# Plain fp32 matmuls for the first two column groups of the second projection, a staging buffer swapped, a bias fill moved, and the last tile reordered in a two-layer encoder

## What is computed

```
p = rmsnorm(x) @ w_in[l]            # mixer a | b | c | cross q | gate
layer 0:  o = softmax(q k^T * 64**-0.5 + bias[dist]) v      # own chunk of 64 and 8 before it
layer 1:  o = rmsnorm(recurrence(q, k, i, log_f))           # state 128 x 128 per head
y = concat(o, cross_attn(xq, mk, mv)) * silu(gate);   x = x + y @ w_out[l]
outputs: final rmsnorm(x), new keys and values, states, memory keys and values
```

## Time and profile before

| | us |
|---|---|
| median of 3 runs (2514.9 to 2525.43) | 2517.48 |
| the profiled execution, its own time | 2513.61 |
| its span, first to last instruction | 2511.7 |
| PE busy / DVE / ACT / POOL in the span | 2404.9 / 1863.4 / 1463.0 / 363.0 |
| mean granted TensorE clock | 0.986 of full |

### The profile page before, as it was taken

The page is one execution under the profiler, slowest core; times in us unless marked ns, Lnnn a source line. Parts: engine busy times, 40 slices in busy tenths (PEclk is TensorE's granted clock), DMA queues, the critical chain, the costliest instruction groups (busy, mean ns, idle before and its releaser), DMA issues. The chain is left out here.

```text
span 2511.7 us, 61163 instructions
## 1 busy us (share of the span) xinstructions
PE 2404.9 (96%) x23733; PEld 2126.7 (85%) x23733; DVE 1863.4 (74%) x3612; ACT 1463.0 (58%) x3337; POOL 363.0 (14%) x584
## 2 busy tenths in 40 slices
PE   8999999999989999999997899999999979999997
PEld 5999999999856777777776898999999968888885
DVE  7899787877655555555555999788798867888884
ACT  4555666655555555555554565676766656666663
POOL 1331000000012111111111232000000021212111
PEclk9999999999999999999999999999999989999998
DMA  6887887789883222222224788777779794443441
GB/s 233 286 294 247 275 277 243 229 249 301 244 250 93 78 62 79 70 72 84 76 77 153 241 292 277 239 250 245 238 252 293 250 277 120 123 139 114 135 129 66
DMA packets 402563, 480.61 MB, mean 191 GB/s; under 512 B 40516, under 2 KB 249212, under 8 KB 402280
## 3 DMA queue, kind: packets, MB, share of 16 engines
q1 hardware_dynamic: 385592, 416.51, 52.5%
q0 software_dynamic: 14848, 55.45, 6.5%
q10 hardware_dynamic: 1840, 4.75, 0.7%
HBM read 329.78 MB, written 151.56 MB: 192 GB/s over the span
## 5 line engine op out<-in xcount | busy, mean ns | idle before, releaser
L1406 PE MATMUL pj_acc<-x_hi,pj_wh 128*128 128x256 f32 (+1 forms) x3136 | 918.4, 293 | 32.7 <-DVE pj_wl L478 30.1
L1406 PE MATMUL pj_acc<-x_lo,pj_wh 128*128 128x256 f32 (+1 forms) x3136 | 906.7, 289 | 0.0
L1406 PE MATMUL pj_acc<-x_hi,pj_wl 128*128 128x256 f32 (+1 forms) x3136 | 906.7, 289 | 0.0
L471 ACT ACTIVATE pj_wh<-pj_wt 128x512 fp32r<-128x512 f32 x728 | 456.5, 634 | 347.5 <-DMA pj_wt<-tsum 251.3
L1406 PEld LDWEIGHTS pj_acc<-x_hi,pj_wh 128*128 128x128 f32 x3136 | 597.5, 191 | 46.3 <-DVE pj_wl L478 43.5
L1406 PEld LDWEIGHTS pj_acc<-x_hi,pj_wl 128*128 128x128 f32 x3136 | 597.9, 191 | 0.0
L1406 PEld LDWEIGHTS pj_acc<-x_lo,pj_wh 128*128 128x128 f32 x3136 | 597.6, 191 | 0.0
L478 DVE SCALAR_TENSOR_TENSOR pj_wl<-pj_wt,pj_wh 128x512 fp32r<-128x512 f32 x728 | 510.3, 716 | 112.6 <-ACT pj_wh L471 98.6
L1259 DVE TENSOR_TENSOR pj_out<-pj_out,pj_acc 128x512 f32<-128x512 f32 (+1 forms) x448 | 319.8, 714 | 87.1 <-PE pj_acc L1406 59.2
L2531 ACT COPY pb_pt<-pb_TP 128x384 f32<-128x384 f32 (+2 forms) x272 | 107.2, 394 | 296.7 <-PE pb_TP L2246 224.1
L2415 DVE COPY pb_pt<-pb_TP 128x256 f32<-128x256 f32 (+2 forms) x266 | 115.8, 435 | 146.7 <-PE pb_TP L2243 133.5
(11 more groups left out here) (341 smaller groups left out, 3872.0 us busy)
## 6 DMA issues: line engine op xcount, KB each, us to landing
pj_wt<-tsum SPq DMA_DIRECT2D x588, 256.0 KB, 3.5
proj<-pj_out SPq DMA_DIRECT2D x112, 512.0 KB, 4.2
tsum<-pj_wt SPq DMA_DIRECT2D x140, 256.0 KB, 3.3
pj_wraw<-in_w_in_dram POOLq DMA_DIRECT2D x24, 1024.0 KB, 6.5
tsum<-pj_wraw SPq DMA_DIRECT2D x56, 256.0 KB, 4.0
hg_x<-x_mid SPq DMA_DIRECT2D x17, 512.0 KB, 3.6
out_dram<-hg_x POOLq DMA_DIRECT2D x17, 512.0 KB, 3.0
pb_gate<-proj SPq DMA_DIRECT2D x16, 512.0 KB, 5.0
```

Source lines behind the costliest of these rows:

```text
L471: nc.scalar.mul(self.hi[j][:], self.source(step), scale_of(c, self.l)).then_inc(self.s_hi, 1)
L1406: ins = nc.tensor.matmul(BANK[j][:, 0:n], a[j][:, k], x.of(y, p, j)[:, k], start=(k == 0 and i == 0), stop=(k == 3 and i == 2))
```

## The change

Four edits, in three stages.

1. **Second projection.** `whole` = 14 steps (groups 0 and 1 of pass 0, layer 1 only) are done in plain fp32: four matmuls a step straight from the sums or raws of x and of the weights. For them no `hi` or `lo` of weights is made. The `hi` of x (terms 2 to 6) go into ACT's loop, the seven `lo` of x into DVE's loop (`LOWS`), each behind the last step that reads its sum. A sum's buffer may now be overwritten only when its store has landed (`s_tst`). The banks of the first transposes (`SPACE`) are permuted.
2. **Sample keys** are staged in the first six blocks of the second gate buffer `gt[1]` in place of `tT`; `load_values(1)` and `load_queries(1)` are issued before that store, the wait on `s_ko` stands before `load_gate(1)`.
3. **Bias fill** of tile 1 at pair MG = 6 in place of pair 3.
4. **Last tile of `prompt_hgrn`**: pieces 8 to 10 behind `outputs`, the others laid between updates and turns; the last job's first half goes to a free bank of `hg_SC`, its second half to `hg_OP`; DVE's state updates go behind `add` and `low_part`; the state's store is issued before the last powers; the last scale and the last store are in two halves, the store on SP.

```diff
+        self.whole = 2 * TERMS * l
@@ add, keep (the same line for sp in keep)
         wait(eng, self.s_mm, step - TERMS + 1)
+        if TERMS <= step < self.whole + TERMS:
+            eng.wait_ge(self.s_tst[j], 16 * c)
@@ low
-        dve.wait_ge(self.s_hi, step + 1)
+        dve.wait_ge(self.s_hi, step + 1 - self.whole)
@@ project
+    LOWS = {5: 1, 6: 3, 8: 0, 10: 2, 12: 4, 13: 5, 14: 6}
-        SPACE = [B1[:], B3[:], B4[:], B52[:, 0], B52[:, 1], B76[:, 0], B76[:, 1], TP[:]]
+        SPACE = [B76[:, 0], B76[:, 1], B1[:], B52[:, 1], B4[:], B52[:, 0], TP[:], B3[:]]
@@ load_raw
-                    pool.wait_ge(w.s_lo, TERMS * (c - 2) + 5)
+                    if TERMS * (c - 2) < w.whole:
+                        pool.wait_ge(w.s_mm, TERMS * (c - 2) + 5)
+                    else:
+                        pool.wait_ge(w.s_lo, TERMS * (c - 2) + 5 - w.whole)
@@ scalar
-                    for j in range(TERMS):
-                        x.high(nc, act, 0, j)
-                        w.high(nc, act, j)
+                    x.high(nc, act, 0, 0)
+                    x.high(nc, act, 0, 1)
...
+                    if l and 1 < t < TERMS:
+                        x.high(nc, act, 0, t)
-                    if t >= 2 and step < STEPS:
+                    if t >= 2 and w.whole <= step < STEPS:
                         w.high(nc, act, step)
@@ vector, in the loop (t = step)
+                    if l and t <= 10 and t in LOWS:
+                        first_low(t)
...
-                    if t >= 5 and step < STEPS:
+                    if t >= 5 and w.whole <= step < STEPS:
                         w.low(nc, dve, step)
+                    if l and t > 10 and t in LOWS:
+                        first_low(t)
@@ tensor
+                        if step < w.whole:
+                            ins = nc.tensor.matmul(BANK[j][:, 0:n], w.source(step)[:, k], x.source(0, j)[:, k],
+                                                   start=(k == 0), stop=(k == 3))
+                            continue
@@ prompt_band, sync
                 load_pair(7)
+                load_values(1)
+                load_queries(1)
...
-                sp.dma_start(v["a_k_sample"][0].rearrange("b s h d -> (b s) (h d)"), tT[:].rearrange("p g n -> p (g n)")
-                             ).then_inc(s_ko, 16)
+                sp.dma_start(v["a_k_sample"][0].rearrange("b s h d -> (b s) (h d)"), staged).then_inc(s_ko, 16)
                 load_weights(3)
-                sp.wait_ge(s_ko, 16)
-                load_values(1)
-                load_queries(1)
                 sp.wait_ge(s_sc, 2 * (PAIRS - 1))
                 load_keys(1)
+                sp.wait_ge(s_ko, 16)
                 load_gate(1)
-                    if T == 1 and p == 3:
+                    if T == 1 and p == MG:
@@ prompt_hgrn
+            return SC[bank(NT - 1, LEVELS - 1)] if (job, half) == (JOBS - 1, 0) else OP
-                            wait(pe, s_xadd, 2 * job + half)
+                            wait(pe, s_xadd, 2 * job if job == JOBS - 1 else 2 * job + half)
+                project(NT - 1, 8, LATE)
                 update(NT - 1, 0)
                 project(NT - 1, LATE, LATE + 2)
                 update(NT - 1, 1)
-                project(NT - 1, LATE + 2, CHUNKS)
                 turn_outputs(NT, 0)
+                project(NT - 1, LATE + 2, LATE + 4)
                 turn_outputs(NT, 1)
+                project(NT - 1, LATE + 4, CHUNKS)
                 project(NT, 0, CHUNKS)
```

More of the change, by code:

```diff
@@ L449, in keep @@
             self.loaded(sp, c)
+            if TERMS <= step < self.whole + TERMS:
+                sp.wait_ge(self.s_tst[j], 16 * c)
         else:
@@ L1300, in _ @@
                     w.add(nc, dve, 1)
-                    w.add(nc, dve, 3)
-                    x.low(nc, dve, 0, 0)
                     dve.wait_ge(x.s_raw, 8)
@@ L1396, in _ @@
                     q, n = pair(step), x.width(p)
-                    pe.wait_ge(w.s_lo, step + 1)
-                    if c == 0:
-                        pe.wait_ge(x.s_lo, TERMS * p + j + 1)
+                    if step < w.whole:
+                        if j in w.PLAIN:
+                            w.loaded(pe, c)
+                        else:
+                            w.summed(pe, c, j)
+                        if c == 0 and j in x.SUMS:
+                            pe.wait_ge(x.s_add, x.MADE[0][j])
+                    else:
+                        pe.wait_ge(w.s_lo, step + 1 - w.whole)
+                        if c == (w.whole // TERMS if p == 0 else 0):
+                            pe.wait_ge(x.s_lo, TERMS * p + (list(LOWS.values()).index(j) if l and p == 0 else j) + 1)
                     if j == 0 or j == 3:
@@ L2678, in bank, with sum_of @@
             return place_of[t, what] % 3
+        def sum_of(job, half):
+            return SC[bank(NT - 1, LEVELS - 1)] if (job, half) == (JOBS - 1, 0) else OP
         def blocks(a):
@@ L2718, in _ @@
                         load_x(t + 1)
+                for half in range(2):
+                    cs = slice(half * 512, half * 512 + 512)
+                    sp.wait_ge(s_out, JOBS + half)
+                    sp.dma_start(v["y_prompt"].rearrange("b (t p) d -> (b t) p d", p=P)[NT - 1][:, cs], xt[NT % 2][:, cs]).then_inc(s_last, 16)
+                sp.wait_ge(s_last, 32)
             @block.gpsimd
@@ L2767, in _ @@
                 power(NT - 1, 1)
-                for job in range(NT - 1, JOBS):
-                    final_power(job)
-                    store(job)
                 pool.wait_ge(s_state, 2 * NT)
                 pool.dma_start(v["b_state_prompt"][0, 0].rearrange("h k v -> k h v"), three(st[:])).then_inc(s_stx[1], 16)
-                pool.wait_ge(s_stx[0], 16 * (JOBS - JOBS // 2))
+                final_power(NT - 1)
+                store(NT - 1)
+                final_power(NT)
+                pool.wait_ge(s_stx[0], 16 * (JOBS - JOBS // 2 - 1))
                 pool.wait_ge(s_stx[1], 16 * (JOBS // 2 + 1))
@@ L3020, in add, with last_scale @@
                     cs = slice(half * 512, half * 512 + 512)
-                    nc.vector.tensor_tensor(xt[job % 2][:, cs], xt[job % 2][:, cs], OP[:], ALU.add).then_inc(s_xadd, 1)
+                    nc.vector.tensor_tensor(xt[job % 2][:, cs], xt[job % 2][:, cs], sum_of(job, half)[:], ALU.add).then_inc(s_xadd, 1)
+                def last_scale(half):
+                    at = NT % 2
+                    cs = slice(half * 512, half * 512 + 512)
+                    dve.wait_ge(s_ldf, 16)
+                    dve.wait_ge(s_frs, JOBS)
+                    nc.vector.scalar_tensor_tensor(out=xt[at][:, cs], in0=xt[at][:, cs], scalar=fr[:, at:at + 1], in1=fg[:, cs],
+                                                   op0=ALU.mult, op1=ALU.mult).then_inc(s_out, 1)
                 def final_mean(job):
```

45 lines of the change are left out of this document (21 added, 24 removed).

## The result

The changed kernel took 2488.8 us, the median of four runs (2482.83 to 2491.52). The kernel before took 2516.2 us beside it, so the ratio is 0.9903 with a 95% interval of 0.9884 to 0.9923: 27.4 us less, 19 to 29 by the interval. The profiled execution took 2482.83 us, with a span of 2481.1 us. The forecast was 2488.5 us. 22 lies in both intervals, 27 only in the first. That the first median came within 0.3 us of the forecast is therefore luck: the direction and most of the mechanism were met, but not every term behind the number.

A forecast was written before the change was run, and what follows sets the result against it. TensorE, busy 2404.9 of 2511.7 us, was taken as the bound. Gains of 9.0 + 3.7 + 8.3 + 6.0 = 27.0 us off a level of 2515.5 gave 2488.5 us, range 2479 to 2503.

The forecast's parts named there:

- start of the second projection: Second projection, steps 0 to 14: fp32 lets PE begin 5.7 us earlier and reach step 14 at 1404.9, gaining 9.0 us.
- band attention, tiles 0 and 1: Tile 0's wait for values goes (3.7 us), tile 1's wait behind POOL and half clock go (8.3 us): 12.0 us.
- end: After the last block copy: earlier last job, no gap between its halves, earlier stores; gain 6.0 us.
- The price of a step: Second projection: a plain fp32 step of four matmuls costs 2.14 us, 0.38 us more than the fp32r step.
- what is late next is `lo` for steps 16 and 17, about 1 us ahead of PE: Second projection after the fp32 steps: DVE's `lo` for steps 16 and 17 has about 1 us of slack.
- The first rival: Band attention: the load stays the limit, tiles 0 and 1 give 3.9 + 1.5 us, time 2495; chance 0.14.
- the two halves: Last job: with its own bank the 1.18 us between the halves becomes 0.24, gaining 0.95 us.
- The stores: End: state stored long before, SP issues the output halves, landing near 2506.4 instead of 2508.55, gaining 2.1 us.
- Everything else of PE's time the change leaves alone: Outside the second projection's start, band attention tiles 0 and 1 and the end, PE's time stays as it was.
- The half clock through all fp32 steps: Second projection rival: fourteen fp32 steps at half clock take 60 us, losing 21 us, time 2518.5; chance 0.02.
- DVE falls behind: Second projection rival: PE idles at step 14 instead of step 0, gain 1 to 3 us, time 2503 to 2510; chance 0.08.
- a wait of over 2 us at steps 14 to 20: Second projection: a new PE wait over 2 us at these steps would show the forecast wrong.

The follow-up runs named there:

- the first edit alone: Kernel before with only the sample keys staged in the second gate buffer and tile 1's values loaded ahead of their store: 2512.3 us, ratio 1.0003.
- the second time: The changed kernel itself, all four edits, timed once more against the kernel before on another chip: 2494.5 us, ratio 0.9923.
- the late `lo`: Changed kernel with the lo of x for terms 4, 5 and 6 put two steps later: 2489.4 us, ratio 0.9910 to the kernel before.

## Why the prediction was right, and where its terms were not

I put the terms beside the means over all kernels that have a stage in the old or in the new form, since one profile can be off by 2 us in a stage.

| term | forecast | in the profiles |
|---|---|---|
| start of the second projection | 9.0 (5.5 to 10) | 7.8 |
| band attention, tiles 0 and 1 | 12.0 (5.4 to 13.2) | 9.0 |
| end | 6.0 (3.5 to 7.5) | 8.5 |
| the recurrence | nothing | -3.5 |
| sum | 27.0 | 21.8 |

**Second projection.** Step 0 began 6.2 us after the start of the transposes in the changed kernel, and at 7.6 to 8.8 in the others. This goes with the transposes at half clock: none of 40 at 6.2 us, 13 at 7.6, 16 at 7.9, 29 at 8.8. I had said 7.7 us. The price of a step, 2.14 us, is the best figure of the prediction: 30.01 us for fourteen are 2.14. By the rule of the Trainium skill (FP8 and Floating Point Precision, section TensorE Precision Notes) of four passes it would have been 2.35, an estimate. The trace shows two records of 0.27 us a matmul, and does not agree in the ratio: an fp32 matmul of 320 columns took 0.54 us, an fp32r one 0.147 (1.76 us for twelve), 3.7 times and not four. To step 14 the gain was 11.5 us by the means, more than the 9.0. The step that failed is "what is late next is `lo` for steps 16 and 17, about 1 us ahead of PE". It was late from step 15 on and gave 3.7 us back. Three things were missing from that schedule. The raw load of group 2 took 9.0 us from its issue, so DVE stood 1.71 us. ACT stood 4.38 us for `pj_nat`, which I had not followed at all, and DVE then 2.13 us for ACT's copy. And the `lo` of x for terms 4 to 6 stood ahead of the `lo` of weights that PE wanted first. Counted to step 22, the experiments give back 0.8 us for the last and 1.0 us for the second.

**Band attention.** Both places paid, and for the reasons given: the values ahead of the store, no POOL wait in tile 1. The full clock came only in part: four of the eight kernels with both edits ran at full clock through tiles 0 and 1, as the changed kernel's first profile did, and four had 3.4 or 6.8 us at half clock behind the new wait for the keys. The w_out blocks did not become late: ACT's casts waited for no load. The mechanism was right and the size off. The stretch of before that I priced was the slowest of four; 11.2 us were gained against it, and 9.0 against their mean. What the prediction did not say is that the first edit alone is worth nothing in the time. I priced tile 0 at 3.7 us by itself, yet POOL waits 2.2 us longer at the bias load for it unless the fill moves too, and the time shows no gain (at most 2 us by the interval). The first rival, that the load stays the limit, is what the kernel with the staging alone shows.

**End.** 8.5 us lie outside the bounds of 3.5 to 7.5. The start of the last job gave 1.3 us (1.7 forecast) and the two halves 2.3 (2.25), so these two terms hold. The stores gave 4.1 us instead of 2.1. The mis-sized term is the landing: the data did land 2.6 us earlier, but I took the landing for the end. Behind it the kernel before went on for 3.5 us and the changed one for 2.0. The half clock behind the old 3.92 us stall, in some profiles 14.6 instead of 13.4 us for the job, makes the rest.

**What was not foreseen.** "Everything else of PE's time the change leaves alone" is the sentence that failed. The edit of the second projection is 113 instructions shorter on PE, and the recurrence pays 3.5 us for it 650 us later. The fp32 edit is therefore worth 4 to 5 us in all, as its own measurement says, about half of my term.

**What made the sum come out.** The errors had both signs: the band attention was priced 3.0 us too high, the second projection 1.2, and the recurrence's 3.5 us were missing, against 2.5 us too little at the end. That leaves 21.8 us. That 27.4 were measured at first, and 19 the second time, is spread and no merit of the terms.

**The rivals.** The half clock through all fp32 steps did not come: the granted clock was 1.00 over them, in all eight kernels. The limit given for it is off by two: for the change to lose its 27 us, the steps would have to spend 54 us at half clock, 27 us of work at full. That DVE falls behind came in part, at steps 15 to 17 instead of step 14. Among what I named as proof of an error, a wait of over 2 us at steps 14 to 20 was the bound, and that sign was set too coarse: three smaller ones stayed under it and still took 3.7 us together with their hand-overs.

## What to carry to other kernels

Judge edits by the stage in which they act, over several profiles: one profile of an unchanged stretch of 45 us differed by up to 4 us from another. When an edit moves a wait, measure up to where both orders run alike again: what the late `lo` won by step 18 was mostly lost by step 22. Two waits in a row behind one full DMA queue are in part one wait: what is gained at the first can be waited for at the second, so remove both. When work is taken off an engine that feeds another, rebuild that engine's order up to the point where both run level again, with the loads and the helpers of other rows in it, and put first what the consumer needs first.

## What the runs showed of the hardware

PE waits for its own code. It comes in packets of 16 KB on a queue of its own, in the changed kernel 192 of them; in dense stretches (123 small matmuls in 1.92 us ahead of the first) PE stops, and it goes on 1.0 to 1.6 us after a packet has landed. In the waits of over 2.5 us the packet starts 0.2 to 0.5 us after PE has stopped, in the shorter ones up to 2.2 us before. One such wait costs 0.6 to 2.9 us. Removing 113 instructions, putting them back, or adding 143 moves these waits: the recurrence took 409, 413, 408 and 415 us in the four forms, the last two with less and more half clock. The Trainium skill (Advanced Engine Details and Errata, section ISA Cache) gives lines of 16 KB, 256 instructions. The packets agree in size; how far ahead they are asked for no run here settles.

DVE and POOL slow one another. DVE's L382 took 2.56 us instead of 1.49 and its L483 1.76 instead of 0.68 beside two sums of POOL, the second of which took 2.17 us instead of 1.4:

```profile
1384.40 1.43 POOL L446 TENSOR_TENSOR pj_wt<-pj_wraw 128x512 f32<-128x512 f32 x1
1386.15 2.17 POOL L446 TENSOR_TENSOR pj_wt<-pj_wraw 128x512 f32<-128x512 f32 x1 [0.32 <-issue]
```

The Trainium skill (SBUF — State Buffer, section "SBUF: two separate sides") says that the two share a port pair which one of them holds for a whole instruction; these rows agree.

In tiles 0 and 1 of the band attention the granted clock fell to half during or right behind each of nine stalls of PE of 2.4 to 4.8 us, for 3.4 to 13.7 us. Behind the new waits of 1.1 to 1.9 us it fell in five kernels and stayed at 1.00 in four; what decides between them no run here shows. Behind the old place of the fill it was 1.00 once the stall was gone. Every version still spends the stretch before the recurrence's dense part at half clock, 0.52 in the changed kernel:

```profile
2027.00:2048.00 21.00, 8.35 (x208) 6.65 (x212) 14.44 (x26) 6.00 (x11) 3.09 (x4) 0.52 0.56 177
```
